# Query projections from high and low parts, and one buffer for each gating input, in the attention of a two-block model

## The reference

```python
def mla_qkv(q_lat, kv_lat, k_rope, q_norm, w_uq, kv_norm, w_ukv, angles):
    q = (rmsnorm(q_lat, q_norm) @ w_uq).reshape(B, T, MLA_HEADS, QK_NOPE + QK_ROPE)   # 384 -> 8 * (128 + 64)
    kv = (rmsnorm(kv_lat, kv_norm) @ w_ukv).reshape(B, T, MLA_HEADS, QK_NOPE + V_DIM) # 256 -> 8 * (128 + 128)
    ...
    q_pe = rope_2d(q_pe, *angles)

def one_block(qi):
    s = jnp.einsum('bqhd,bkhd->bhqk', qi, k) * ATTN_SCALE
    p = jax.nn.softmax(s, axis=-1)
    return jnp.einsum('bhqk,bkhd->bqhd', p, v)
```

## Time and profile before

| what | value |
|---|---|
| median of 3 runs | 3679.38 us (3674.17 to 3680.17) |
| the profiled execution's own time | 3680.69 us |
| its span in the trace | 3678.9 us |
| mean granted clock of TensorE | 0.944 |
| busy: PE, PEld, DVE, ACT, POOL | 3319.2, 2697.5, 1875.8, 1421.6, 684.8 us |
| the attention of the first block | from 620.6 to about 1248 us of the span |
| PE records on `att_wq` | 192 (24 a head), busy 86.1 us |

### The profile page before, as it was taken

One profiled execution on the slowest core, in us unless ns is written; L12 is line 12 of the kernel. 1 busy time (PEld: TensorE's weight loads), 2 busy tenths in 40 slices (PEclk: granted clock), 3 DMA queues, 4 the chain that ended last, 5 costly groups with the idle time before them and its releaser, 6 DMA issues. The chain is left out here.

```text
span 3678.9 us, 42963 instructions
## 1 busy us (share of the span) xinstructions
PE 3319.2 (90%) x17029; PEld 2697.5 (73%) x17029; DVE 1875.8 (51%) x2598; ACT 1421.6 (39%) x1943; POOL 684.8 (19%) x454
## 2 busy tenths in 40 slices
PE   6989998999999799794999999599989896998989
PEld 3767775778778687573887877488878685887967
DVE  3356775444344354646788888414325432252543
ACT  4222231333333244432777776421135334112530
POOL 2100001011111245201545555300000003000000
PEclk8999999999999899896999999799999897999989
DMA  5426555101010132325999997411130034113102
GB/s 186 118 88 200 172 172 171 32 31 36 25 32 18 58 112 57 129 102 207 365 390 380 387 381 288 148 51 37 33 108 15 17 111 145 53 46 96 27 24 80
DMA packets 248689, 471.50 MB, mean 128 GB/s; under 512 B 25455, under 2 KB 137072, under 8 KB 248492
## 3 DMA queue, kind: packets, MB, share of 16 engines
q1 hardware_dynamic: 232904, 410.88, 32.3%
q0 software_dynamic: 15264, 57.70, 4.7%
q10 hardware_dynamic: 324, 0.15, 0.0%
HBM read 406.12 MB, written 55.22 MB: 125 GB/s over the span
## 5 line engine op out<-in xcount | busy, mean ns | idle before, releaser
L2353 DVE TENSOR_TENSOR exp_wl<-wts_raw,exp_wh 128x2048 fp32r<-128x2048 f32 x144 | 394.4, 2774 | 105.8 <-ACT exp_wh L2313 105.8
L2313 ACT ACTIVATE exp_wh<-wts_raw 128x2048 fp32r<-128x2048 f32 x192 | 368.0, 1919 | 196.3 <-PE exp_gate L2242 64.6
L2656 PE MATMUL pr_ps<-l_h_high,pr_wh 128*128 128x512 f32 (+1 forms) x896 | 335.9, 375 | 22.5 <-DVE pr_wl L2795 22.5
L2657 PE MATMUL pr_ps<-l_h_low,pr_wh 128*128 128x512 f32 (+1 forms) x896 | 330.8, 369 | 0.0
L2658 PE MATMUL pr_ps<-l_h_high,pr_wl 128*128 128x512 f32 (+1 forms) x896 | 329.8, 368 | 0.0
L696 PE MATMUL in_ps<-iw_h_high,in_wh 128*128 128x512 f32 (+1 forms) x696 | 274.3, 394 | 13.9 <-DVE in_wl L874 13.9
L2211 POOL TENSOR_TENSOR exp_wl<-wts_raw,exp_wh 128x2048 fp32r<-128x2048 f32 x48 | 229.4, 4780 | 265.0 <-ACT exp_wh L2313 265.0
L697 PE MATMUL in_ps<-iw_h_low,in_wh 128*128 128x512 f32 (+1 forms) x696 | 264.0, 379 | 0.0
L698 PE MATMUL in_ps<-iw_h_high,in_wl 128*128 128x512 f32 (+1 forms) x696 | 263.6, 379 | 0.0
L2795 DVE TENSOR_TENSOR pr_wl<-pw_raw,pr_wh 128x512 fp32r<-128x512 f32 x88 | 60.1, 692 | 358.2 <-ACT pr_wh L2717 356.9
L2656 PEld LDWEIGHTS pr_ps<-l_h_high,pr_wh 128*128 128x128 f32 x896 | 170.2, 190 | 54.1 <-DVE pr_wl L2795 23.2
(11 more groups left out here) (514 smaller groups left out, 7491.5 us busy)
## 6 DMA issues: line engine op xcount, KB each, us to landing
wts_raw<-in_w_e_gate SPq DMA_DIRECT2D x64, 1024.0 KB, 9.7
wts_raw<-in_w_e_up SPq DMA_DIRECT2D x64, 1024.0 KB, 9.0
wts_raw<-in_w_e_down SPq DMA_DIRECT2D x64, 1024.0 KB, 7.8
in_mw<-in_w_mod SPq DMA_DIRECT2D x80, 512.0 KB, 4.6
pw_raw<-in_w_in SPq DMA_DIRECT2D x88, 256.0 KB, 2.9
iw_raw<-in_w_in SPq DMA_DIRECT2D x74, 256.0 KB, 4.6
mod_w<-in_w_mod SPq DMA_DIRECT2D x4, 2048.0 KB, 11.8
wo_w<-in_w_out SPq DMA_DIRECT2D x2, 4096.0 KB, 21.2
```

Of the source, the lines that this page charges most:

```text
L2313: act.activation(wh[:, m % RING], raw[:, m % RAW_RING], ACT.Copy).then_inc(high, 1)
L2353: dve.tensor_tensor(wl[:, m % RING], raw[:, m % RAW_RING], wh[:, m % RING].bitcast(F32), ALU.subtract).then_inc(low, 1)
L2656: nc.tensor.matmul(out, wh[:, slot, k, :], hi, start=h == 0 and k == 0, stop=False)
L2657: nc.tensor.matmul(out, wh[:, slot, k, :], lw, start=False, stop=False)
```

## The change

The query weights and the latent rows are split into high and low parts (`wqh`, `wql`, `lat_hi`, `lat_lo`), and a query projection adds three float32r products for each float32 product. The latent rows are split once, at the start. The weights of a head are split during the step of tile 3 of the head before (`SPLIT_AT`): ScalarE's `weights_high` stands behind its copies of that step, VectorE's `weights_low` behind its `copy_last`. The query weights are loaded one head earlier, once `wq` has been split. Each gating input has one buffer, and `s1` has none: it is loaded into the rows of `g.yT` in which the head's output is to stand. VectorE's first copy of an output of a head (in `copy_last(head, 1)`) therefore waits for `x_gated`, and SP's loads for a head wait for `y_gated` of the head before.

```diff
@@ -998 +998 @@ attention
         wq = ph.sb("wq", [P, QL, QK + ROPE])
+        wqh, wql = ph.sb("wqh", [P, QL, QK + ROPE], FR), ph.sb("wql", [P, QL, QK + ROPE], FR)
+        lat_hi, lat_lo = ph.sb("lat_hi", [P, QL, N_LAT], FR), ph.sb("lat_lo", [P, QL, N_LAT], FR)
...
-        sm = ph.sb("sm", [P, 2, N_LAT])
-        xc, s1 = ph.sb("xc", [P, 2, N_LAT]), ph.sb("s1", [P, 2, N_LAT])
+        sm, xc = ph.sb("sm", [P, 1, N_LAT]), ph.sb("xc", [P, 1, N_LAT])
...
+        SPLIT_AT = 3
@@ -1067 +1070 @@ sync
+                def query_weights(head):
+                    if head:
+                        sp.wait_ge(wq_low, head)
+                    sp.dma_start(wq[:, :, 0:QK], q_cols[:, :, head % HEADS * QK:(head % HEADS + 1) * QK]).then_inc(wq_in, 16)
+                    sp.dma_start(wq[:, :, QK:], q_cols[:, :, head % HEADS * QK + NOPE:(head % HEADS + 1) * QK]).then_inc(wq_in, 16)
+
+                def load(head):
+                    if head:
                         b, earlier = use(head - 1, PROJ - 1)
                         sp.wait_ge(full[b], earlier + 1)
-                    sp.dma_start(wq[:, :, 0:QK], q_cols[:, :, ds(head * QK, QK)]).then_inc(wt_in, 16)
-                    sp.dma_start(wq[:, :, QK:], q_cols[:, :, ds(head * QK + NOPE, ROPE)]).then_inc(wt_in, 16)
...
-                    if head >= 2:
-                        sp.wait_ge(y_gated, head - 1)
-                    sp.dma_start(sm[:, j:j + 1, :], g.sm_dram[ds(head, 1)].rearrange("o p n -> p o n")).then_inc(sm_in[j], 16)
-                    sp.dma_start(xc[:, j:j + 1, :], g.xc_dram[ds(head, 1), :, N_CTX:].rearrange("o p n -> p o n")).then_inc(sm_in[j], 16)
-                    sp.dma_start(s1[:, j:j + 1, :], g.s1_dram[ds(head, 1)].rearrange("o p n -> p o n")).then_inc(sm_in[j], 16)
+                    query_weights(head + 1)
+                    if head:
+                        sp.wait_ge(y_gated, head)
+                    sp.dma_start(sm[:, 0, :], g.sm_dram[head]).then_inc(sm_in, 16)
+                    sp.dma_start(xc[:, 0, :], g.xc_dram[head][:, N_CTX:]).then_inc(sm_in, 16)
+                    sp.dma_start(g.yT[:, head, :], g.s1_dram[head]).then_inc(sm_in, 16)
+
+                query_weights(0)
                 for head in range(HEADS):
-                    load(head, head % 2, head == 0)
+                    load(head)
@@ gpsimd: gate(head)
-                    pool.tensor_tensor(x, x, s1[:, j:j + 1, :], ALU.mult).then_inc(x_gated, 1)
+                    pool.tensor_tensor(x, x, y, ALU.mult).then_inc(x_gated, 1)
@@ -1114 +1124 @@ tensor
                 def project(head, j):
-                    pe.wait_ge(wt_in, 48 * (head + 1))
+                    def queries(b, cols, c):
+                        return accumulate(nc, tb[:, b, :], [
+                            (w[:, k, cols], lat[:, k, HALVES[c]]) for k in range(QL)
+                            for w, lat in ((wqh, lat_hi), (wqh, lat_lo), (wql, lat_hi))])
+
+                    pe.wait_ge(lat_low, QL)
+                    pe.wait_ge(wq_low, head + 1)
                     for c in range(2):
-                        into_bank(head, ROPE_USE + c, lambda b: accumulate(nc, tb[:, b, :], [
-                            (wq[:, k, NOPE:], g.ql[:, k, HALVES[c]]) for k in range(QL)]))
+                        into_bank(head, ROPE_USE + c, lambda b: queries(b, slice(NOPE, QK + ROPE), c))
...
+                    pe.wait_ge(wt_in, 16 * (head + 1))
@@ -1246 +1261 @@ scalar
+                def weights_high(head):
+                    act.wait_ge(wq_in, 32 * (head + 1))
...
+                    act.activation(wqh[:], wq[:], ACT.Copy).then_inc(wq_high, 1)
+
                 def one(head, j, first):
...
                         copy_turned(h, t, 1)
+                        if t == SPLIT_AT:
+                            weights_high(head + 1)
+
+                for k in range(QL):
+                    act.activation(lat_hi[:, k, :], g.ql[:, k, :], ACT.Copy).then_inc(lat_high, 1)
+                weights_high(0)
@@ -1306 +1333 @@ vector
+                def weights_low(head):
+                    dve.wait_ge(wq_high, head + 1)
+                    dve.tensor_tensor(wql[:], wq[:], wqh[:].bitcast(F32), ALU.subtract).then_inc(wq_low, 1)
...
                     dve.wait_ge(full[b], earlier + 1)
+                    if t == 1:
+                        dve.wait_ge(x_gated, head + 1)
                     if not (first and t == 0):
                         copy_output(b, *before(head, t)).then_inc(y_out, 1)
...
                             copy_last(*before(h, t), first)
+                        if t == SPLIT_AT:
+                            weights_low(head + 1)
                     copy_last(head, LT - LAG - 1, first)
 
+                for k in range(QL):
+                    dve.wait_ge(lat_high, k + 1)
+                    dve.tensor_tensor(lat_lo[:, k, :], g.ql[:, k, :], lat_hi[:, k, :].bitcast(F32), ALU.subtract).then_inc(lat_low, 1)
+                weights_low(0)
```

More of the change, by code:

```diff
@@ L1015, in attention @@
         tb = ph.ps("tb", [P, 2, BANK])
-        wt_in = ph.sem("wt_in")
+        wt_in, wq_in = ph.sem("wt_in"), ph.sem("wq_in")
         full = [ph.sem(f"full{b}") for b in range(2)]
@@ L1025, in attention @@
         x_skip, x_gated, y_mul = ph.sem("x_skip"), ph.sem("x_gated"), ph.sem("y_mul")
-        sm_in = [ph.sem(f"sm_in{j}") for j in range(2)]
+        sm_in = ph.sem("sm_in")
+        lat_high, lat_low, wq_high, wq_low = (ph.sem(n) for n in ("lat_high", "lat_low", "wq_high", "wq_low"))
+        SPLIT_AT = 3
         ROPE_USE, NOPE_USE, ROT_USE, KEY_USE, VAL_USE, PROJ, TURN = 0, 2, 4, 6, 9, 12, 3
@@ L1069, in _ @@
             def _(sp):
-                def load(head, j, first):
-                    if not first:
+                q_cols = io["w_uq"].rearrange("(k p) n -> p k n", p=P)
+                kv_cols = io["w_ukv"].rearrange("(k p) n -> p k n", p=P)
+                def query_weights(head):
[3 more added lines that the diff above has]
+                    sp.dma_start(wq[:, :, QK:], q_cols[:, :, head % HEADS * QK + NOPE:(head % HEADS + 1) * QK]).then_inc(wq_in, 16)
@@ L1072, in load @@
+                def load(head):
+                    if head:
                         b, earlier = use(head - 1, PROJ - 1)
                         sp.wait_ge(full[b], earlier + 1)
-                    q_cols = io["w_uq"].rearrange("(k p) n -> p k n", p=P)
-                    kv_cols = io["w_ukv"].rearrange("(k p) n -> p k n", p=P)
-                    sp.dma_start(wq[:, :, 0:QK], q_cols[:, :, ds(head * QK, QK)]).then_inc(wt_in, 16)
-                    sp.dma_start(wq[:, :, QK:], q_cols[:, :, ds(head * QK + NOPE, ROPE)]).then_inc(wt_in, 16)
@@ L1078, in load @@
-                    sp.dma_start(wkv[:], kv_cols[:, :, ds(head * (NOPE + VD), NOPE + VD)]).then_inc(wt_in, 16)
-                    if first:
+                    sp.dma_start(wkv[:], kv_cols[:, :, head * (NOPE + VD):(head + 1) * (NOPE + VD)]).then_inc(wt_in, 16)
+                    if head == 0:
                         sp.dma_start(cos[:], io["t_cos"]).then_inc(cs_in, 16)
                         sp.dma_start(sin[:], io["t_sin"]).then_inc(cs_in, 16)
-                    if head >= 2:
-                        sp.wait_ge(y_gated, head - 1)
@@ L1087, in _, with gate @@
+                    sp.dma_start(sm[:, 0, :], g.sm_dram[head]).then_inc(sm_in, 16)
+                    sp.dma_start(xc[:, 0, :], g.xc_dram[head][:, N_CTX:]).then_inc(sm_in, 16)
+                    sp.dma_start(g.yT[:, head, :], g.s1_dram[head]).then_inc(sm_in, 16)
+                query_weights(0)
                 for head in range(HEADS):
-                    load(head, head % 2, head == 0)
+                    load(head)
             @block.gpsimd
             def _(pool):
-                def gate(head, j, first):
-                    pool.wait_ge(sm_in[j], (head - j) * 24 + 48)
-                    x = xc[:, j:j + 1, :]
+                def gate(head):
+                    pool.wait_ge(sm_in, 48 * (head + 1))
+                    x, y = xc[:], g.yT[:, ds(head, 1), :]
@@ L1097, in gate @@
                     pool.wait_ge(x_skip, head + 1)
-                    pool.tensor_tensor(x, x, s1[:, j:j + 1, :], ALU.mult).then_inc(x_gated, 1)
+                    pool.tensor_tensor(x, x, y, ALU.mult).then_inc(x_gated, 1)
                     pool.wait_ge(y_out, LT * (head + 1))
-                    y = g.yT[:, ds(head, 1), :]
-                    pool.tensor_tensor(y, y, sm[:, j:j + 1, :], ALU.mult).then_inc(y_mul, 1)
+                    pool.tensor_tensor(y, y, sm[:], ALU.mult).then_inc(y_mul, 1)
                     pool.wait_ge(x_gated, head + 1)
@@ L1105, in _ @@
                 for head in range(HEADS):
-                    gate(head, head % 2, head == 0)
+                    gate(head)
                 pool.wait_ge(y_gated, HEADS)
@@ L1116, in project @@
                 def project(head, j):
-                    pe.wait_ge(wt_in, 48 * (head + 1))
+                    def queries(b, cols, c):
```

(14 more changed lines are left out.)

## The result

The changed kernel takes 3759.27 us in the median of 4 runs (3757.86 to 3761.19), against 3679.45 us before. The ratio is 1.0225, with a 95% interval of 1.0212 to 1.0238: it is 80 us slower. The forecast was 3756.5 us in a range of 3727 to 3790.

What follows compares the result with a forecast made beforehand. TensorE and what it waits for were taken as the bound. Gating 46.0, split 22.4, products -15.8, start 0.3 and clock 24.2 made 77.1 us; 3680.7 + 77.1 - 1.3 = 3756.5 us, range 3727 to 3790.

Steps and rivals of the forecast that it cites:

- The products: Query projections at a head's start: 36 split products take 8.3 us instead of 10.30, saving 15.8 us in eight heads.
- The split wait: Step of tile 3: VectorE's difference waits for ScalarE's late weight copy, delaying TensorE 2.8 us a head, 22.4 in eight.
- The gating wait: Step of tile 2, heads 1 to 7: VectorE's first output copy waits for the gating loads; TensorE stops, 46.0 us.
- 1.77 us slower already: Odd heads before the change: slow normalisation beside GpSimd's skip product, so TensorE's stop there is 5.8 us, not 7.6.
- The clock: TensorE's lower clock after waits: 15.4 us for seven long ones, 8.8 for eight of 2.8 us, 24.2 together.
- The caution: Short waits taken at 1.1 us of clock each, between nothing and 1.7, as both drops seen had another idle time nearby.
- The rows on VectorE beside GpSimd: Odd heads' normalisation: its 1.70 us delay was close to the skip product's 1.89, agreeing in direction with the exclusion rule.
- a clock that costs nothing: Rival for TensorE's clock: both waits happen, but it stays at 2.4 GHz; 3732 us, chance 0.12.
- slower loads: Rival for the gating inputs: the third load takes 9.4 us as in head 0; 3782 us, chance 0.12.
- only the split waits: Rival for the gating step: inputs arrive before the output copy wants them; 3695 us, chance 0.06.
- the cover decides: Rival for VectorE: both new instructions fall into its 2.8 us idle time and hold nothing back; 3656 us, chance 0.03.
- the products save nothing: Rival for the projections: split products lose their 0.231 us pace, 15.8 us more; 3772 us, chance 0.03.

Runs made afterwards that it cites:

- the experiment: The kernel before with one buffer shared by sm and the third gating input, plain float32 projections: 3680.93 us, stage 16.1 us longer than with split products and neither wait.
- the filled stops: Changed kernel with unused products in TensorE's long and short stops: 3735.66 us, stage 22.2 us shorter than the changed kernel's.
- the short stops alone: Changed kernel with the third gating input loaded into sm's buffer, so VectorE's output copy waits for nobody: 3692.13 us.
- the long ones alone: Changed kernel with ScalarE's copy of the weights one step earlier, at tile 2: 3726.92 us.
- both undone: Changed kernel with the third gating input in sm's buffer and ScalarE's weight copy one step earlier; split products stay: 3664.42 us, ratio 0.9968 to before.

## Why the prediction was right

**The products:** 8.3 us in six of the heads, forecast 8.3. In heads 0 and 4, which began at the lower clock, they took 10.3 and 9.9. The sum had 15.8 us for all; the experiment gave 16.1.

**The split wait:** forecast 2.8 us a head, measured 2.73 in heads 0 and 1 and 2.80 in the others, 22.3 us. Its parts came as costed: 0.83 us for the copy (0.82), 0.96 for the difference (0.95), and TensorE's turn late by what VectorE was late.

**The gating wait:** the round trip was forecast at 15.9 us and was 15.9 in the mean of seven heads (15.4 to 17.0). The landing of the third load decided the spread: GpSimd started 5.3 to 6.9 us after its issue.

**Where this term was mis-sized:** it said 3 x 7.6 + 4 x 5.8 = 46.0 us, because odd heads were "1.77 us slower already". The stops after, from the timeline of weight loads, are 7.61, 8.75, 7.20, 7.27, 7.46, 8.01 and 7.51 us, 53.8 in all. From that goes 1.77 that head 1 had lost before, so 52.0: the term was 6.0 too small. With 7.6 in all seven it would have been 53.2. The step at fault is the reading of the pattern. Heads 1, 3 and 5 were longer in the trace of before (75.6, 75.9 and 76.0 us from projection to projection, the others 74.1 to 75.1), but only head 1 had the slow normalisation, and only there did TensorE want the turn 10.80 us after GpSimd's start; it was 9.03 to 9.06 in the six others. The trace of the kernel before, in the timeline of weight loads:

```profile
751.50 0.42 PEld L1160 LDWEIGHTS att_tb<-g_ident,att_p 128*128 128x128 f32 x4 [1.77 <-DVE att_p L1282]
...
926.76 0.30 PEld L142 LDWEIGHTS att_tb<-g_ql,att_wq 128*128 128x128 f32 x2 [1.81 <-issue]
...
1077.00 0.30 PEld L142 LDWEIGHTS att_tb<-g_ql,att_wq 128*128 128x128 f32 x2 [1.92 <-issue]
```

The other two long intervals hold an idle time at the start of heads 4 and 6, where the hardware loop over pairs of heads turns, put down to "issue" and to no wait. It is there in the changed kernel too (962.47 and 1136.24), and no row ties it to GpSimd. Two causes of nearly the same size looked like one pattern.

**The clock:** forecast 24.2 us; the filled stops gave 22.2. The total came out, but its split into 15.4 for the long stops and 8.8 for the short was a guess on bounds, and the windows of the changed kernel have 13.1 and 13.4 at most. A short stop there cost the 1.7 us of the windows before, the upper bound, and a long one 1.9, less than the 2.2 taken. That the two errors cancel is luck. The caution, that both drops seen in head 0 had a second idle time close to them, is borne out only in part: without the long stops three of the eight short ones left the clock alone, but the one of head 0, with no long stop near it, lowered it in both kernels. What decides it no run here shows.

The 7.0 us by which the two waits are more than their sum can't be put down to this. With the short stops alone their windows lose 8.2 us instead of 13.4, but with the long ones alone theirs lose 17.5 instead of 13.1, and three falls of the clock where the loop turns, one in the profile of the changed kernel and two in that of both undone, come to 5 us. It stays open whether there is anything beyond the noise.

**The sum again, from what was measured:** 52.0 + 22.3 - 16.1 + 0.1 (start: TensorE's first load 5.59 us behind SP's first issue, 5.52 before) + 22.2 = 80.5, against 80.0. The gating term was 6.0 too small and the clock's 2.0 too large, which partly cancel; in the profiles 2.6 us came off in the rest of the kernel, where the forecast had no change, so the forecast time is closer than its terms.

**The rows on VectorE beside GpSimd:** the forecast took 1.70 us for the normalisation's delay and 1.89 for the skip product's length as near to each other. More can be read: the slow normalisation ended at 751.45, 0.68 us after the skip product (748.88 + 1.89), and the seven slow ones with both waits undone all end 0.67 to 0.69 us after theirs. In the row of before VectorE's record starts 0.02 us ahead of GpSimd's, so that VectorE was the second to issue can't be read from it.

**The rivals:** a clock that costs nothing fell with the filled stops, slower loads with the landing times, "only the split waits" and "the cover decides" with the rows above, and "the products save nothing" with the 16.1 us.

## What to carry to other kernels

An instruction that fits an engine's idle time by length may still stop the kernel by its place: ask which engine's which instruction it waits for, and whether that one is behind something late. Here one word, the step at which ScalarE's copy of 0.83 us stood, was worth 32 us, and the buffer chosen for one input was worth 68, at the same memory.

A buffer that is also an output's place ties the next load to the output's reader and writer; walk the whole round trip (gate, issue, landing, use, copy) and set it against the time until its result is wanted. To save memory, share a buffer between two inputs that are used one after the other, away from the engine that sets the pace.

Count a stall of TensorE with its lower clock behind it, 1.9 to 2.5 us for each of the long ones here and 1.7 for a short one behind which the clock fell; and before a periodic difference is put down to one cause, look at each of its periods.

## What the runs showed of the hardware

A stop of TensorE of 2.8 us lowered the granted clock in five of eight cases by itself and in eight of eight beside the long stops, to 0.72 to 0.74 over the next 6.0 us each time. Filling the eight that stood alone gave back 4.7 us. Stops of 4.7 to 5.1 us cost as much clock as stops of 7.2 to 8.8.

VectorE's difference of two tiles in SBUF (768 columns) takes 0.95 us, but 2.52 to 2.62 us when it is issued beside GpSimd's product of two tiles, and its normalisation in place takes 1.2 to 1.9 us instead of 0.89. How long depends on when it starts, but not when it ends: with both waits undone each of the seven slow normalisations ends 0.67 to 0.69 us after GpSimd's skip product, and each of the seven slow differences 0.81 or 0.82 us after the product with the third input (the one at 895.31 at 897.92, the product at 897.10). That is nearly as if each had waited for GpSimd and then run, for which they need 0.89 and 0.95 us. The Trainium skill ("SBUF — State Buffer", Who interferes with whom) gives the reason as one pair of ports that the two engines share under an exclusive lock. By it a two-input instruction such as the difference takes its second input through the shared read interface. In the step shown GpSimd's product had begun first both times (892.28 and 894.25) and VectorE was the one that was late, which agrees with a lock. Idle time on VectorE took up the longer difference; of the longer normalisations 0.2 to 0.9 us each reached TensorE, 3.7 in seven heads.
